# One table load per pair of roots, and the output scaling placed one fill later, in the recurrence of a three-layer block

## The reference, cut to what matters

```python
def step(state, inp):                       # per chunk, all heads
    qi, ki, vi, gi = inp
    cum = jnp.cumsum(gi, axis=2)
    o_inter = jnp.einsum('bhtk,bhkv->bhtv', qi * jnp.exp(cum), state)
    ...
    o_intra = jnp.einsum('bhts,bhsv->bhtv', scores, vi)
    ...
    return new_state, o_inter + o_intra
...
o = o * lax.rsqrt(jnp.mean(o * o, axis=-1, keepdims=True) + NORM_EPS)
o = o.reshape(b, s, D_MODEL) * out_norm.astype(jnp.float32) * jax.nn.silu(g.astype(jnp.float32))
return o.astype(h.dtype) @ w_out
```

## Time and profile before

| | |
|---|---|
| time, median of 3 runs | 2879.76 us (2875.03 to 2884.04) |
| profiled execution, its own time | 2881.03 us |
| its span | 2878.9 us |
| TensorE matmul busy | 2713.2 us, 94% |
| VectorE busy | 1109.9 us, 39% |
| ScalarE busy | 893.7 us, 31% |
| GpSimd busy | 1002.6 us, 35% |
| recurrence within the span | about 2119 to 2444 us |

### The profile page before, as it was taken

One profiled execution on the slowest core, in us unless ns is written; L12 is line 12 of the kernel. 1 busy time (PEld: TensorE's weight loads), 2 busy tenths in 40 slices (PEclk: granted clock), 3 DMA queues, 4 the chain that ended last, 5 costly groups with the idle time before them and its releaser, 6 DMA issues.

```text
span 2878.9 us, 30584 instructions
## 1 busy us (share of the span) xinstructions
PE 2713.2 (94%) x13119; PEld 2269.6 (79%) x13119; DVE 1109.9 (39%) x1429; ACT 893.7 (31%) x1150; POOL 1002.6 (35%) x220
## 2 busy tenths in 40 slices
PE   6889999999889999999999999999988998899998
PEld 6777888776768788888887988888887787777787
DVE  3745414445463635511114242111264444534424
ACT  1222114555421212522224333222333333422222
POOL 0333344222233334344444333344432221343342
PEclk7899999999999999999999999999999999899999
DMA  5555433111164635222322322323221111222321
GB/s 196 199 189 205 161 99 116 63 59 59 59 241 139 226 126 197 81 96 95 100 91 88 104 80 81 103 88 103 88 77 59 59 45 45 74 88 88 103 88 59
DMA packets 251997, 310.53 MB, mean 108 GB/s; under 512 B 7197, under 2 KB 231214, under 8 KB 251863
## 3 DMA queue, kind: packets, MB, share of 16 engines
q1 hardware_dynamic: 248874, 304.93, 31.7%
q10 hardware_dynamic: 2988, 3.66, 0.4%
HBM read 306.44 MB, written 4.74 MB: 108 GB/s over the span
## 4 chain that ended last, share of the span: by engine, by line
PE 81%; DVE 8%; ACT 4%; DMA 3%; POOL 3%; issue 2%; SPq 1%; DVEq 0%; ACTq 0%
PE bank L1616 23%; PE bank L1617 22%; PE bank L1618 22%; POOL w_lo_t L686 3%; DMA w_raw<-in_ffn_wg 2%; PE bank L1561 2%; DVE scr L1220 2%; PE bank L1640 1%; ACT w_hi_t L839 1%; PE bank L1641 1%; PE bank L1725 1%; PE bank L1642 1%; ACT w_hi_t L845 1%; DVE h_lo L1204 1%; PE bank L1748 1%
## 5 line engine op out<-in xcount | busy, mean ns | idle before, releaser
L686 POOL TENSOR_TENSOR w_lo_t<-w_raw,w_hi_t 128x2048 fp32r<-128x2048 f32 x216 | 1002.4, 4642 | 1845.8 <-ACT w_hi_t L839 1096.3
L1616 PE MATMUL bank<-h_hi,w_hi_t 128*128 128x512 f32 (+1 forms) x2160 | 843.8, 391 | 60.8 <-POOL w_lo_t L686 33.7
L1617 PE MATMUL bank<-h_lo,w_hi_t 128*128 128x512 f32 (+1 forms) x2160 | 828.1, 383 | 0.0
L1618 PE MATMUL bank<-h_hi,w_lo_t 128*128 128x512 f32 (+1 forms) x2160 | 827.6, 383 | 0.0
L1616 PEld LDWEIGHTS bank<-h_hi,w_hi_t 128*128 128x128 f32 x2160 | 415.7, 192 | 153.2 <-POOL w_lo_t L686 39.2
L1616 PE MATMUL bank<-act_hi,w_hi_t 128*128 128x512 f32 (+1 forms) x1264 | 486.4, 385 | 45.1 <-POOL w_lo_t L686 19.2
L1617 PE MATMUL bank<-act_lo,w_hi_t 128*128 128x512 f32 (+1 forms) x1264 | 478.9, 379 | 0.0
L1618 PE MATMUL bank<-act_hi,w_lo_t 128*128 128x512 f32 (+1 forms) x1264 | 478.3, 378 | 0.0
L1617 PEld LDWEIGHTS bank<-h_lo,w_hi_t 128*128 128x128 f32 x2160 | 416.3, 193 | 77.9 <-issue 3.1
L1618 PEld LDWEIGHTS bank<-h_hi,w_lo_t 128*128 128x128 f32 x2160 | 415.1, 192 | 78.1
L845 ACT CAST w_hi_t<-w_raw 128x2048 fp32r<-128x2048 f32 x104 | 197.9, 1903 | 484.6 <-DMA w_raw<-in_ffn_wg 218.6
(11 more groups left out here) (233 smaller groups left out, 2247.9 us busy)
## 6 DMA issues: line engine op xcount, KB each, us to landing
scr<-in_ada_w SPq DMA_DIRECT2D x128, 512.0 KB, 6.6
w_raw<-in_ffn_wg SPq DMA_DIRECT2D x44, 1024.0 KB, 5.2
w_raw<-in_ffn_wu SPq DMA_DIRECT2D x44, 1024.0 KB, 5.2
w_raw<-in_ffn_wd SPq DMA_DIRECT2D x32, 1024.0 KB, 5.1
w_raw<-in_mlp_w SPq DMA_DIRECT2D x32, 1024.0 KB, 5.4
w_raw<-in_hgrn_w_in SPq DMA_DIRECT2D x16, 1024.0 KB, 5.3
w_raw<-in_ffn_wd SPq DMA_DIRECT2D x16, 768.0 KB, 4.4
w_raw<-in_attn_w_qkv SPq DMA_DIRECT2D x12, 1024.0 KB, 5.1
```

Of the source, the lines that this page charges most:

```text
L686: nc.gpsimd.tensor_tensor(w_lo_t[:, s], w_raw[:, s], w_hi_t[:, s].bitcast(F32), ALU.subtract).then_inc(w_lo, 1)
L1616: pe.matmul(dst, w_h, m_h, start=first, stop=False)
L1617: pe.matmul(dst, w_h, m_l, start=False, stop=False)
L1618: return pe.matmul(dst, w_l, m_h, start=False, stop=last)
```

## The change: what it does

```diff
@@ hgrn_sequence @@
                 if j < 3:
                     seq.append(("osum", j))
                     for b in range(2):
-                        after(1 + b, ("hn", j, b))
-                        after(2 + b, ("lo", j, b))
+                        after(2 + b, ("hn", j, b))
+                        after(3 + b, ("lo", j, b))
@@ hgrn_act @@
                 elif step[0] == "osum":
                     j = step[1]
+                    act.preload_act_table_set("natural_log_exp_and_others")
                     for b in range(2):
                         act.wait_ge(o_ss, 8 + 2 * j + b + 1)
```

## The result

The changed kernel takes 2862.27 us (median of 4 runs, 2858.37 to 2864.21), against 2880.07 for the kernel before in the same set (4 runs, 2875.03 to 2884.04): ratio 0.9937, interval 0.9918 to 0.9957, 17.8 us less. The forecast was 2870, range 2863 to 2876. The direction was right, and the time lies 0.7 us under the range. The profiled execution took 2864.21, its span is 2862.1 us.

What follows compares the result with a forecast made beforehand. TensorE, holding 81% of the chain, was taken to bound the kernel, with waits passed on through VectorE's order. Boundaries 2.4, clock 1.5 and end 6.3 sum to 10.2 us off 2879.76, giving 2869.6, forecast as 2870, range 2863 to 2876.

Steps and rivals of the forecast that it cites:

- VectorE's multiply is held by GpSimd; a wait of 3.15 us stays: Before level 1 at three boundaries: multiply held until GpSimd's L686 ends, so TensorE's wait falls from 4.05 to 3.15 us.
- The first rival: At the boundaries: VectorE not held by GpSimd, the whole 4.05 us wait and its slow clock go, 2852; chance 0.07.
- its milder form: At the boundaries: multiply only slowed to twice its 1.22 us, 3.0 a boundary, 2864 or less; counted within the 0.07.
- The removed loads are worth nothing at the boundaries: Three loads removed per boundary free 3.8 us on ScalarE, but nobody on the path waits for the roots: worth 0.
- Level 3 late by 0.1 us: Head 1's scaling (1.40 us) ahead of level 3's update exceeds 1.36 us slack, so level 3 is about 0.1 us late.
- The clock gives back 0.5 each: Behind each of three boundaries, the shorter wait returns 0.5 us of slow clock (0 to 1.8 possible), 1.5 in all.
- The end, 6.3 us, of which 2.5 from the clock: End of the recurrence: three loads removed between the last roots gain 3.83 us, and full clock behind gains 2.5.
- The second rival: At the end: clock falls all the same or weight tile's chain is less tight; 3.8 or less remains, 2875; chance 0.16.
- The slower rival: At three boundaries: a later update's L1090 slips behind L686 and is held, level 5 waits 3.8 us, 2884; chance 0.06.
- The sum, 10.2 us: Whole program: 2.4 from boundary waits, 1.5 from clock there and 6.3 from the end make 10.2 us.
- the base and its scatter: Start of the forecast: profiled execution 2881.03, 1.3 us over the median 2879.76; about 2 us scatter in a median of three.

Runs made afterwards that it cites:

- e4: The changed kernel with level 1's multiply written ahead into a buffer of its own: 2833.11 us, ratio 0.9852 against the kernel before.
- e3: The kernel before with the new order of steps alone, table loads as before: 2869.51 us, ratio 0.9981.
- e2: The kernel before with the table load alone, old order of steps: 2866.18 us, ratio 0.9966.
- e7: The kernel before with the table load for the last pair alone: 2867.85 us, ratio 0.9973.
- e8: e4 with the scaling back at its old place, table loads kept: 2852.25 us, ratio 0.9917 against the kernel before.
- e11: The changed kernel run once more, unaltered: 2864.93 us, ratio 0.9964 against the kernel before.

## Why the prediction was right or wrong, step by step

- **VectorE's multiply is held by GpSimd; a wait of 3.15 us stays.** Right, to 0.01 us, in all four traces of the changed kernel. e4 shows that this hold, and not the copy or the bank, is what kept the wait. The first rival (not held) fell; so did its milder form, twice the length. One reading behind it was loose: the earlier trace rows show L1136 not "in the middle" of L686 but across its end (2219.84 to 2220.59, L686 until 2220.48). That an operation which reads a bank isn't held is shown better by e4's rows, in the middle of L689.
- **The removed loads are worth nothing at the boundaries.** With the new order right: e3 without them has the same waits of 3.15. With the old order they give 0.29 a boundary (e2).
- **Level 3 late by 0.1 us.** Right (0.22 against 0.12). The three boundaries gave 0.8, 1.5 and 0.8 us in three traces, against 0.80 each worked out without the clock.
- **The clock gives back 0.5 each.** Mis-sized and not a constant: in three traces it gave about 0.7 us over all three boundaries, in the fourth 4.8.
- **The end, 6.3 us, of which 2.5 from the clock.** Right: 6.3 us between the same two roundings in the changed kernel and in e7. The second rival fell.
- **The slower rival** didn't happen in the changed kernel, but its mechanism is real: e8's pair 2.
- **The sum, 10.2 us.** The number came out in three of four traces, with 13.7 in the fourth, but that it came out so exactly is luck: 2.4 + 0.7 + 6.3 are 9.4, and the other 0.8 us lie behind the end, where the prediction had no term. Where those 0.8 come from no run isolates.
- **What failed: the base and its scatter.** The step is "That execution lies 1.3 us over the median 2879.76" together with "about 2 us of scatter in a median of three". That execution lay some 5 us over the medians of the later sets. The first trace of the kernel before is the latest of eight at the start of the recurrence, by 5 to 8 us, and the four runs of its set have a median 4 us over those of the later sets (2875.5, 2876.8 and 2876.0, from 15 to 20 runs each). Single runs of this one kernel spread over 8 to 14 us within each later set. From 2876.0 the sum of 10.2 gives 2865.8, and the changed kernel's four medians are 2862.3, 2862.3, 2864.6 and 2864.9. So the 17.8 us of the first set are some 11 to 14 of change and about 4 of a base that stood high. Whether it stood high by chance in four runs or for that set as a whole no run shows. Why the rest isn't exactly 10.2 is partly the clock: behind the same waits the changed kernel's varied in e11, and pair 0's 2.8 us of extra slow clock occurred in two of four traces of before and in none of the seven of altered kernels whose pair 0 is unchanged. That is too few to say whether it is chance, and the remainder isn't separated from scatter.

## What to carry to other kernels

Before counting an operation at its usual length in its new place, look at what GpSimd does at that time: level 1's multiply, which reads two SBUF tiles, lasted until the end of the GpSimd operation that it started behind, so what is worth moving is the work that isn't held, or the held work into a stretch in which GpSimd is idle. Here the move of the order gave 0.9 us of wait at each boundary, and taking the held multiply away (e4) gave the other 3.15. A wait in front of a restart is worth more than its length on TensorE, but what the clock adds differs from one execution to the next. When a change worth a few tenths of a per cent is forecast in absolute time, the base's own scatter, here 8 us at one instruction in four traces of one program, belongs into the range.

## What the runs showed of the hardware that was not expected

- Whether a VectorE operation slips ahead of GpSimd's or is held for its whole length can turn on about 0.1 us: started 0.05 us ahead of the record of L686 it took 0.69 us, started 0.07 us behind it took 4.98 (e8). The Trainium skill (GPSIMD Engine Reference, Key points) names the contention for instructions with two SBUF inputs; these rows agree, and show that the later one waits for the other's end.
- The start of the record doesn't always decide, and the hold goes both ways. In the kernel before, eight back-to-back operations on two large tiles (L1315) ran in 5.39 us although the last two started 0.18 and 0.85 us behind the start of L686's record, and L686 took 6.05 us instead of 4.6. What decides between the two cases isn't shown. Nor are two large tiles needed: L1025, which reads one large tile and a small one, took 3.73 us behind an L686, and 0.35 elsewhere. VectorE and GpSimd, kernel before:

```profile
1218.71 5.39 DVE L1315 SCALAR_TENSOR_TENSOR x<-x,vec,scr 128x512 f32<-128x512 f32 x8
1222.50 6.05 POOL L686 TENSOR_TENSOR w_lo_t<-w_raw,w_hi_t 128x2048 fp32r<-128x2048 f32 x1 [8.75 <-ACT w_hi_t L845]
...
531.82 0.35 DVE L1025 TENSOR_SCALAR hidden<-hidden,small 128x128 f32<-128x128 f32 x1
608.14 3.73 DVE L1025 TENSOR_SCALAR hidden<-hidden,small 128x128 f32<-128x128 f32 x1
607.21 4.58 POOL L686 TENSOR_TENSOR w_lo_t<-w_raw,w_hi_t 128x2048 fp32r<-128x2048 f32 x1 [11.09 <-ACT w_hi_t L839]
```

- The slow clock behind a wait of the same length and the same work can be 0.62 or 0.81 over 9 us, in one and the same program: 3.4 or 1.7 us lost. Of the changed kernel's four executions, one (e11) shows the second in all three places; the other three show 0.62, 0.63 and 0.69.
